# Two heads as two halves of the matmul array, and a reordered opening, in a hybrid decoder layer

## The reference

```python
mod = silu(c) @ w_ada + b_ada                       # shift1, scale1, gate1, shift2, scale2, gate2
h = rms_norm(x, g_norm1) * (1 + scale1) + shift1
z = h @ w_in                                        # qa ka va qb kb vb qi ki wi fl ga gb
# mixer A: index scores, top-k keys, attention with ALiBi; 8 heads of 64
s = einsum('bths,bth->bts', relu(einsum('bthd,bsd->bths', qi, ki) * 64**-0.5), wi)
oa = sparse_attend(qa, ka[sel], va[sel])            # sel = top_k(masked s)
# mixer B: forgetting attention; 8 heads of 64
ob = softmax(qb @ kb.T / 8 + Fq - Fk, causal) @ vb  # F = cumsum(log_sigmoid(fl + b))
merged = sigmoid(ga) * (oa @ w_o_a) + sigmoid(gb) * (ob @ w_o_b)
x = x + gate1 * (merged @ w_out)
h2 = rms_norm(x, g_norm2) * (1 + scale2) + shift2
y = x + gate2 * (square(relu(h2 @ w_up)) @ w_down)
```

## Time and profile before

| | us |
|---|---|
| median of 3 runs | 1118.53 |
| lowest and highest run | 1115.49, 1121.29 |
| the profiled execution | 1120.04 |
| its span, which all positions below count from | 1118.2 |
| PE busy | 1007.4 (90%) |
| DVE busy | 577.5 (52%) |
| ACT busy | 409.9 (37%) |
| POOL busy | 183.4 (16%) |
| first weight matmul starts | 44.61 |
| span of pair 2 (slot 0 to slot 0) | 36.8 |
| span of pair 7 | 35.9 |

### The profile page before, as it was taken

The page is one execution under the profiler, slowest core; times in us unless marked ns, Lnnn a source line. Parts: engine busy times, 40 slices in busy tenths (PEclk is TensorE's granted clock), DMA queues, the critical chain, the costliest instruction groups (busy, mean ns, idle before and its releaser), DMA issues.

```text
span 1118.2 us, 19588 instructions
## 1 busy us (share of the span) xinstructions
PE 1007.4 (90%) x7336; PEld 911.4 (82%) x7336; DVE 577.5 (52%) x1295; ACT 409.9 (37%) x818; POOL 183.4 (16%) x127
## 2 busy tenths in 40 slices
PE   5889988898989888649989999599989999998998
PEld 4687777787778778637489999589989999998998
DVE  2634899767575662563048844664433234442232
ACT  3355454444555442112065444344421124431111
POOL 4303223322342223320002322000000000000000
PEclk9799999999999999779979999799999999998999
DMA  9521521312222225774626665223323233332322
GB/s 323 165 79 32 163 76 48 87 45 62 56 67 57 59 57 160 246 233 135 207 85 198 193 201 173 76 57 95 94 76 94 83 87 93 94 94 75 88 64 77
DMA packets 186184, 124.51 MB, mean 111 GB/s; under 512 B 16499, under 2 KB 170163, under 8 KB 186116
## 3 DMA queue, kind: packets, MB, share of 16 engines
q1 hardware_dynamic: 185986, 123.50, 36.8%
q10 hardware_dynamic: 130, 0.10, 0.0%
HBM read 116.99 MB, written 6.59 MB: 111 GB/s over the span
## 4 chain that ended last, share of the span: by engine, by line
PE 74%; DVE 9%; DMA 5%; issue 4%; SPq 3%; ACT 3%; POOL 2%; ACTq 0%; DVEq 0%; POOLq 0%
PE bank L842 19%; PE bank L843 19%; PE bank L844 19%; PE bank L922 3%; PE bank L904 3%; DMA qbc<-q_d 3%; PE bank L1069 2%; PE bank L913 2%; POOL prod L772 1%; SPq L557 1%; DVE w_lo L1658 1%; PE bank L888 1%; PE bank L885 1%; PE bank L884 1%; PE bank L887 1%
## 5 line engine op out<-in xcount | busy, mean ns | idle before, releaser
L842 PE MATMUL bank<-h_hi,w_hi 128*128 128x260 f32 x1360 | 410.5, 302 | 29.0 <-issue 14.2
L843 PE MATMUL bank<-h_lo,w_hi 128*128 128x260 f32 x1360 | 394.8, 290 | 0.0
L844 PE MATMUL bank<-h_hi,w_lo 128*128 128x260 f32 x1360 | 393.9, 290 | 0.0
L842 PEld LDWEIGHTS bank<-h_hi,w_hi 128*128 128x128 f32 x1360 | 267.6, 197 | 37.9 <-issue 30.7
L843 PEld LDWEIGHTS bank<-h_lo,w_hi 128*128 128x128 f32 x1360 | 267.7, 197 | 4.1 <-issue 2.9
L844 PEld LDWEIGHTS bank<-h_hi,w_lo 128*128 128x128 f32 x1360 | 267.2, 196 | 0.0
L742 POOL TENSOR_TENSOR w_lo<-raw,w_hi 128x1024 fp32r<-128x1024 f32 x44 | 104.9, 2383 | 396.1 <-ACT w_hi L1259 229.6
L842 PE MATMUL bank<-u_hi,w_hi 128*128 128x260 f32 x512 | 147.0, 287 | 7.7 <-DVE u_lo L2046 7.7
L2031 DVE TENSOR_TENSOR w_lo<-raw,w_hi 128x1024 fp32r<-128x1024 f32 x62 | 76.0, 1226 | 146.2 <-ACT w_hi L1490 146.2
L843 PE MATMUL bank<-u_lo,w_hi 128*128 128x260 f32 x512 | 146.3, 286 | 0.0
L844 PE MATMUL bank<-u_hi,w_lo 128*128 128x260 f32 x512 | 146.3, 286 | 0.0
(11 more groups left out here) (319 smaller groups left out, 1384.0 us busy)
## 6 DMA issues: line engine op xcount, KB each, us to landing
raw<-in_w_in SPq DMA_DIRECT2D x44, 512.0 KB, 3.7
raw<-in_w_ada SPq DMA_DIRECT2D x32, 512.0 KB, 4.1
raw<-in_w_up SPq DMA_DIRECT2D x32, 512.0 KB, 3.8
raw<-in_w_down SPq DMA_DIRECT2D x32, 512.0 KB, 3.6
ada<-in_w_ada SPq DMA_DIRECT2D x4, 2048.0 KB, 13.6
kv<-in_cache_k_b SPq DMA_DIRECT2D x16, 256.0 KB, 3.1
qbc<-q_d SPq DMA_DIRECT2D x16, 256.0 KB, 4.1
kv<-in_cache_k_a SPq DMA_DIRECT2D x16, 256.0 KB, 3.4
```

The lines of the kernel that those rows point to most:

```text
L842: mm(out, hi[:, k, :], x_h, start=first and k == ks[0], stop=False)
L843: mm(out, hi[:, k, :], x_l, start=False, stop=False)
L844: end = mm(out, lo[:, k, :], x_h, start=False, stop=last and k == ks[-1])
```

## The change

Scores: `q_pad` gives way to `q_fm`, q of both heads without zeros. Each score product runs over 64 rows, the two heads' products one after the other into banks 4 and 5, both in the even slot of a pair of slots. A unit is now head U%2 and query block U%8//2, so the heads alternate. The products of index scores go in pairs in the same way. `values(U)` is now made for both heads and one query block at a time, in odd slots, in matmuls of 128 columns whose outputs are the two halves of bank 7. `store_back` and the stores of `q_idx` are one ACT instruction where they were two, and POOL zeroes neither buffer.

Opening: tile 0 is one DMA of 80 columns, and an ACT copy puts fl in its place; tile 2 is loaded ahead of the small constants. x is turned in two parts, chunks 0 to 3 ahead of the first c product and 4 to 7 between the second c product and the first weight tile. DVE scales all eight chunks, four and four. The first two weight tiles take chunks 0 to 3, then c products 2 and 3 with their turns follow on PE, then chunks 4 to 7.

```diff
@@ tile_dmas, dma_count
             if i == T_SMALL:
-                return [(dst[:, :, 0:HD], w_in_v[:, :, KI:KI + HD]), (dst[:, :, 64:64 + H], w_in_v[:, :, WI:WI + H]),
-                        (dst[:, :, ROW_FL:ROW_FL + H], w_in_v[:, :, FL:FL + H])]
+                return [(dst[:, :, 0:GA - KI], w_in_v[:, :, KI:GA])]
@@ gpsimd
-            pool.memset(q_idx[:, :, :], 0.0).then_inc(zeroed, 1)
...
-            for j in range(XN_DVE, NCH):
-                pool.tensor_tensor(xn[:, j, :], x_t[:, j, :], rs_all[:, :], ALU.mult).then_inc(xn_pool, 1)
...
-            pool.memset(q_pad[:, :, :, :], 0.0).then_inc(zeroed, 1)
@@ tensor, opening
+            turn_x(0)
+            turn_x(1)
             pe.wait_ge(c_landed, 16 * 5)
...
+            turn_x(2)
+            turn_x(3)
+            pe.wait_ge(cond_ready, 1)
+            mod_product(0)
             pe.wait_ge(diag_ready, 1)
...
+            pe.wait_ge(rs_all_ready, 1)
+            mod_turn(0)
+            mod_product(1)
+            turn_x(4)
+            turn_x(5)
+            mod_turn(1)
+            turn_x(6)
+            turn_x(7)
@@ first_tiles
                 for k in range(NCH):
+                    if k == 4 and not n:
+                        mod_product(2)
+                        mod_turn(2)
+                        mod_product(3)
+                        mod_turn(3)
@@ scores, values
             def scores(U):
-                p, hh, qb = U // 8, U // 4 % 2, U % 4
+                p, _, qb = unit(U)
                 if U >= 2:
-                    pe.wait_ge(lg_ready, U - 1)
+                    pe.wait_ge(lg_ready, U)
...
-                mm(bank[4 + U % 2][:, 0:width(qb)], q_pad[:, p % 2, hh, qb * P:(qb + 1) * P],
-                   k_fm[:, p % 2, 0:width(qb)], start=True, stop=True).then_inc(s_done, 1)
+                for hh in range(2):
+                    rows = slice(64 * hh, 64 * hh + 64)
+                    mm(bank[4 + hh][:, 0:width(qb)], q_fm[rows, p % 2, qb * P:(qb + 1) * P],
+                       k_fm[rows, p % 2, 0:width(qb)], start=True, stop=True).then_inc(s_done, 1)
...
-            def values(p, hh):
-                pe.wait_ge(pt_ready, 8 * p + 4 * hh + 4)
...
-                for kb in range(QB):
-                    last = mm(bank[7][64 * hh:64 * hh + 64, kb * P:SEQ], v_tok[:, p % 2, kb, 64 * hh:64 * hh + 64],
-                              p_t[:, hh, kb, kb * P:SEQ], start=kb == 0, stop=kb == QB - 1)
+            def values(U):
+                p, _, qb = unit(U)
+                pe.wait_ge(pt_ready, U + 2)
...
+                for kb in range(qb + 1):
+                    for hh in range(2):
+                        rows = slice(64 * hh, 64 * hh + 64)
+                        last = mm(bank[7][rows, qb * P:(qb + 1) * P], v_tok[:, p % 2, kb, rows],
+                                  p_t[:, qb % 2, hh, kb, :], start=kb == 0, stop=kb == qb)
@@ index_scores
                 if n >= 2:
-                    pe.wait_ge(idx_relu, n - 1)
+                    pe.wait_ge(idx_relu, n)
@@ pair loop on tensor
-                    for n in range(3 * s, 3 * s + 3):
+                    for n in range(3 * s + s % 2, 3 * s + 3, 2):
                         index_scores(n)
...
-                if 0 <= U < N_UNITS:
+                if 0 <= U < N_UNITS and U % 2 == 0:
...
-                if s == 6 and 1 <= p <= N_PAIRS:
-                    values(p - 1, 0)
-                if s == 2 and p >= 2:
-                    values(p - 2, 1)
+                if 0 <= U - 5 < N_UNITS and U % 2:
+                    values(U - 5)
@@ scalar
             mod_rows(0)
+            act.wait_ge(raw_landed[0], landed_value(0))
+            link(A(raw[:, 0, :, ROW_FL:ROW_FL + H], raw[:, 0, :, FL - KI:GA - KI], ACT.Copy))
+            round_w(0)
             mod_rows(1)
-            round_w(0)
+            store_x(4)
             round_w(1)
+            store_x(6)
...
-                if s == 2 and p >= 2:
+                if s == 3 and p >= 2:
                     round_o(p - 2)
@@ vector
             mod_add(0)
+            rest_w(0)
+            store_x(5)
             mod_add(1)
-            rest_w(0)
             rest_w(1)
-            dve.wait_ge(xn_dve, XN_DVE)
+            dve.wait_ge(xn_dve, 4)
             first_half(0)
+            store_x(7)
+            store_xs(1)
...
+            for j in range(4, NCH):
+                scale_x(j)
             mod_add(2)
             mod_add(3)
```

More of the change, by code:

```diff
@@ L203, in layer @@
         z = new("z", [P, 3, SEQ])
-        q_pad = new("q_pad", [P, 2, 2, SEQ])
+        q_fm = new("q_fm", [P, 2, SEQ])
+        place["at"] += 4096
         k_fm = new("k_fm", [P, 2, SEQ])
@@ L216, in layer @@
         pt_at = place["at"]
-        p_t = new("p_t", [P, 2, QB, SEQ])
+        p_t = new("p_t", [P, 2, 2, QB, P])
+        place["at"] += 8192
         ts_b, ts_at, ts_end = sb("ts_b", [NS, 4, SEQ])
@@ L528, in _ @@
             load_ada(3)
+            load(2)
             for half in range(2):
@@ L782, in _, with turn_x, mod_product, mod_turn @@
             pe.wait_ge(consts, 1)
+            pe.wait_ge(xs_landed, 16)
+            for g in range(2):
+                pe.wait_ge(x_landed[g], 16)
+            def turn_x(j):
+                if j == 7:
+                    pe.wait_ge(mod_row_ready, 1)
+                elif j >= 4:
+                    pe.wait_ge([xt_act, xt_dve][j % 2], (j - 4) // 2 + 1)
+                tr(bank[6][:, 8 * j:8 * j + 8], x_stok[:, j * P:(j + 1) * P], ident[0:NS, 0:NS])
+                for t in range(QB):
+                    last = tr(bank[X_BANK[j]][:, t * P:(t + 1) * P], x_tok[:, t, j * P:(j + 1) * P], ident[:, :])
+                last.then_inc(xt_done, 1)
+            def mod_product(t):
+                if t >= 2:
+                    pe.wait_ge(mod_row_ready, t - 1)
+                if t == 2:
+                    pe.wait_ge(xt_dve, 4)
+                pe.wait_ge(ada_landed[t], 16)
+                for r in range(2):
+                    for j in range(4):
+                        last = mm(bank[2 + t % 2][32 * j:32 * j + 32, :], cond_t[:, 4 * r + j, :], ada[:, t, 4 * r + j, :],
+                                  start=r == 0, stop=r == 1)
+                last.then_inc(mod_done, 1)
+            def mod_turn(u):
+                pe.wait_ge(mod_row_ready, u + 1)
+                if u:
+                    pe.wait_ge(mod_ready, u)
+                for q in range(4):
+                    last = mm(bank[7][:, 192 + 36 * u + 9 * q:192 + 36 * u + 9 * q + 9], mod_row[:, u % 2, q * P:(q + 1) * P], fold[:, :],
+                              start=True, stop=True)
+                last.then_inc(mod_turned, 1)
+            turn_x(0)
+            turn_x(1)
             pe.wait_ge(c_landed, 16 * 5)
@@ L956, in index_scores @@
                 if n >= 2:
-                    pe.wait_ge(idx_relu, n - 1)
-                mm(bank[4 + n % 2][:, 0:width(qb)], q_idx[:, h, qb * P:(qb + 1) * P], ki2[:, 0:width(qb)],
-                   start=True, stop=True).then_inc(idx_done, 1)
+                    pe.wait_ge(idx_relu, n)
+                for hh in range(2):
+                    rows = slice(64 * hh, 64 * hh + 64)
+                    mm(bank[4 + hh][:, 0:width(qb)], q_idx[rows, h // 2, qb * P:(qb + 1) * P], ki2[rows, 0:width(qb)],
+                       start=True, stop=True).then_inc(idx_done, 1)
             def side_step(e):
@@ L1231, in _ @@
             act.wait_ge(rs_spread, 1)
-            A(rs_all[:, SEQ:T], bank[1][:, 0:NS], ACT.Copy)
-            A(rs_all[:, 0:SEQ], bank[0][:, :], ACT.Copy).then_inc(rs_all_ready, 1)
+            A(rs_all[:, SEQ:T], bank[7][:, 136:136 + NS], ACT.Copy)
+            A(rs_all[:, 0:SEQ], bank[3][:, :], ACT.Copy).then_inc(rs_all_ready, 1)
             def mod_rows(t):
@@ L1296, in exps @@
             def exps(U):
[L1297 removed]
+                w = width(U % 8 // 2)
                 act.wait_ge(lg_ready, U + 1)
@@ L1376, in _ @@
                     c = i - T_QI
-                    if i == T_QI:
-                        act.wait_ge(zeroed, 2)
-                    A(q_idx[0:64, 2 * c, lo:hi], bank[half + 4 * par(i)][0:64, 0:hi - lo], ACT.Copy)
-                    last = A(q_idx[64:128, 2 * c + 1, lo:hi], bank[half + 4 * par(i)][64:128, 0:hi - lo], ACT.Copy)
+                    last = A(q_idx[:, c, lo:hi], bank[half + 4 * par(i)][:, 0:hi - lo], ACT.Copy)
                     if half == 1:
@@ L1581, in _ @@
             dve.wait_ge(rs_all_ready, 1)
-            dve.wait_ge(xt_act, 4)
-            dve.wait_ge(xt_dve, 5)
-            for j in range(XN_DVE):
-                dve.tensor_tensor(xn[:, j, :], x_t[:, j, :], rs_all[:, :], ALU.mult).then_inc(xn_dve, 1)
+            dve.wait_ge(xt_act, 2)
+            dve.wait_ge(xt_dve, 2)
+            dve.wait_ge(xs_dve, 1)
+            for j in range(4):
+                scale_x(j)
             def mod_add(t):
@@ L1883, in _ @@
                         normalize(p, s // 2 - 1)
-                if s == 3 and p >= 2:
+                if s == 4 and p >= 2:
```

148 lines of the change are left out of this document (61 added, 87 removed).

## The result

The changed kernel takes 1125.77 us (median of 11 runs, 1120.62 to 1130.97). The kernel before, in 11 runs beside it, takes 1119.16 us. The ratio is 1.0052, 95% interval 1.0028 to 1.0076: it is **slower by half a per cent**, where 1107 us had been forecast. The profiled execution took 1125.87 us with a span of 1123.9.

What follows compares the result with a forecast made beforehand. PE and its waits were taken to bound the kernel, DVE pairs 1 and 2. Terms -8.8, -1, +0.5 and -2 summed to -11.3 us, from 1118.53 to 1107 us; forecast band 1100 to 1113, range 1094 to 1121.

Steps and rivals of the forecast that it cites:

- Scores and values: Pair loop: halved products run side by side, scores -2.1 us and values -1.9 us a pair.
- rival 3: Scores and values: the halves don't run side by side, so the kernel is slower, 1139 us; chance 0.1.
- The switches: Pair loop: 8 excursions into the 64 column form instead of 2, +1.0 us a pair, bounds 0 and 1.6.
- The waits of slots 5 and 7: Pair loop: PE waits 2.4 and 2.7 us for ACT's store, 5.1 a pair against 3.0 before, +2.1 us a pair.
- pairs 3 to 8: Pair loop where PE and its waits bound: scores, values, switches and waits less cover, -8.8 us.
- The clock: Pair loop: three losses go, 4.8 us, and new waits bring 3 x 1.6, so the clock comes out even.
- Rival 2: Slots 5 and 7: low clock follows every new wait, +12.8 us, 1120; chance 0.18 together with half of rival 3.
- a clock below 0.93 in pairs 5 to 8: Pair loop: one of the signs named as showing the prediction wrong, a granted clock under 0.93 there.
- The index scores: Ahead of pair 1: halved products save 8 us but pairs wait for both banks, +0.5 us, bounds -0.5 and +3.
- The opening: Start to the end of tiles 0 and 1: they end at about 57 instead of 58.8, -2 us, bounds -5.5 and +3.
- Pairs 1 and 2: Pair loop where DVE bounds: its work is unchanged, slack 1 to 2 us each, -1 us for both.
- the pair loop: All pairs: -8.8 us for pairs 3 to 8 and -1 for the first two, -9.8 us.

Runs made afterwards that it cites:

- e5: Changed kernel with 8 matmuls whose result nobody reads ahead of the turned probabilities in slots 5 and 7; 1113.79 us, ratio 0.9941.
- e3: Changed kernel with 16 matmuls whose result nobody reads ahead of the turned probabilities in slots 5 and 7; 1127.85 us, ratio 1.0087.
- e9: Changed kernel with 8 unread matmuls in slots 5 and 7 and index scores one head at a time; 1107.27 us, ratio 0.9873.
- e6: Changed kernel with index scores one head at a time again, each on its half of the array; 1120.45 us, ratio 1.0013.
- e8: Changed kernel with p_t stored ahead of exps in even slots, rest_o first in slot 4, and single index scores; 1100.35 us, ratio 0.9825.
- e4: Kernel before with only the opening of the changed kernel; 1119.74 us, ratio 0.9990.
- e12: Kernel before with 8 matmuls whose result nobody reads in slot 5 of each pair; 1116.56 us, ratio 0.9967.
- e2: Kernel before with ACT's store of p_t ahead of exps in every slot; 1110.63 us, ratio 0.9923.
- e11: Changed kernel, single index scores; unread matmuls (slots 5, 7) in pairs 1 and 2, early p_t store and rest_o from pair 3; 1103.73 us, ratio 0.9861.

## Why the prediction was wrong, point by point

- **Scores and values: right in the products.** The scores of a pair take 0.42 + 0.63 + 0.85 + 1.06 = 3.0 us: 1.67 ns a column for both heads together and 0.21 us for each of the four excursions (the way into the 64 row form and back). One head alone took 0.86 / 512 = 1.68 ns a column, so the overlap is full, and rival 3, halves that don't overlap, is out. The values take 2.8 us (2.7 forecast): 0.37, 0.59, 0.81 and 1.02 us for 4, 8, 12 and 16 instructions, that is 0.15 us for the excursion and 0.054 for each instruction.
- **The switches: mis-sized.** Part of an excursion's price stands in the step ahead of it, which I had not looked at. One transpose of the probabilities takes 0.11 us ahead of the padded scores of the kernel before (352.01 to 352.12), and 0.20 us ahead of the new scores (360.70 to 360.90) and of the values (364.52 to 364.72):

```profile
352.01 0.27 PE L913 MATMUL bank<-ident,lg 128*128 128x128 f32 x1
```

```profile
360.70 0.27 PE L928 MATMUL bank<-ident,lg 128*128 128x128 f32 x1
360.90 0.70 PE L919 MATMUL bank<-k_fm,q_fm 64*128 64x256 f32 x4
...
364.52 0.27 PE L928 MATMUL bank<-ident,lg 128*128 128x128 f32 x1
364.72 1.09 PE L942 MATMUL bank<-p_t,v_tok 128*64 128x128 f32 x16
```

So an excursion costs 0.30 us for the scores and 0.24 for the values, and the eight of a pair 2.2 us. Less the two of before, which are some 0.25 us each, that is about +1.7, where +1.0 had been forecast with a bound of 1.6. PE's whole work in a pair can be read from e5's trace, which is at the full clock, with idle time and filling taken off. In pairs 5, 6 and 7 it is 2.3, 2.3 and 1.9 us shorter than before, where 3.0 had been forecast.

- **The waits of slots 5 and 7: right in place and sum.** 16 places with some 35 us in sum had been named, 15 with 34.9 came. In pair 7 they are 2.05 and 2.40 us, 4.5 a pair instead of 5.1; in slot 5 of pairs 1 and 2 they are 3.57 and 2.91, though no wait of 3.3 had been expected. By the windows of the earlier trace rows, pairs 3 to 8 held 19.6 us of waits before and not 17.9.
- **The clock: the step that failed.** "I price this as one loss in every second pair, 3 x 1.6, which makes the clock come out even." The trace has 15 slow half tiles with 20.7 us against 6 with 9.1: 11.6 us on the wrong side, and e3, e5 and e9, where the waits are filled, have none of them in the loop. I had put the point from which an idle time is followed by the low level at about 2.5 us, from one row of the opening and the harmless waits of 1.7. In the trace after, 2.05 us are enough in three of the four waits of that length, in slot 5 of pairs 5 to 8 (the half tiles behind 300.84 and 372.87 lost 1.6 each, that behind 336.15 lost 1.0, that behind 409.05 nothing), and even a wait of 1.86 us (345.66) has a half tile behind it that loses 1.0, where another of 1.86 (310.49) has none. The length does not decide it alone. In the trace after, 13 of the 15 waits have a slow half tile right behind them; in e6, with the same loop and 15 waits of 1.86 to 3.58 us, only nine; before, one of the six waits of 3.27 us and more has none (331.79), which the prediction doesn't mention; and in e8 one of 1.56 us (139.44) is followed by a loss of 1.6. What decides it is not shown. Rival 2 had this mechanism, with 12.8 us for it, and a chance of 0.18; it should have been the forecast. The condition I had named as one that would prove the prediction wrong, a clock below 0.93 in pairs 5 to 8, is met at 0.91 in pairs 6 and 7.
- **The index scores: wrong by size.** +0.5 had been forecast with bounds to +3, and 3.9 came, about one of it a slow half tile at its end. (The stretch before is also longer than I had put it: 24 times 0.77 is 18.4 us and not 17.) That DVE can't start before 125.6 held only as long as PE was there by then; in the trace after, PE's last index score ends at 125.9 behind a wait of 2.60 us. The waits of a pair for both banks were walked through at 1.1, 1.9 and 2.9 us, but the halved work was credited against them, although DVE and ACT, whose relus and sums are not halved, set the pace.
- **The opening: right in its steps, worth nothing in the time.** `first_half(0)` starts at 31.44 (29.7 forecast), tiles 0 and 1 end at 60.05 in this trace and at 55.6 in e8's (57 forecast). e4 can't be told from the kernel before.
- **Pairs 1 and 2:** 36.7 and 38.3 instead of 35.9 and 36.8, where -1 for both had been taken. Their waits of up to 3.57 us have slow half tiles behind them, which DVE's bound did not hide.

Where the forecast and the spans of the two traces part, stretch by stretch: the opening +2.3 instead of -2, the index scores +3.9 instead of +0.5, the pair loop +3.5 instead of -9.8, the rest -4.0 instead of 0. That is +5.7 instead of -11.3, and 13.3 of the 17.0 us between them lie in the loop. Within pairs 3 to 8 (-8.8 forecast, +1.2 measured), again with e5 as the measure of the work at the full clock, the work shrank by about 13.3 us and not 18.0, the waits grew by 5.8 (1.5 of it ahead of the last spread) and not 9.2, and the low clock took 8.7 more and not 0. So the two misses in work and waits nearly cancel, and the clock is what is left.

What the halves are worth without the clock can be seen in the pair loop of two pairs of traces: e9 against e12, both with filling, 293.7 against 301.4 us (e12 has two slow half tiles left in it, with 2.7 us, and e9 none), and e8 against e2, both with the early store, 288.2 against 295.5 (with about as much loss in slow half tiles, 4.5 and 4.8). That is -7.7 and -7.3 us where -9.8 had been forecast for the loop. Their ratios differ by some 10 and 11 us, but of the two differences in span 2.8 and 3.0 us lie in the opening, and in the second 4.4 behind the loop. What stays open is why the clock falls behind the wait in pair 3 of e11 and only 6 us later in e8; a single profile of each doesn't settle it.

## What to carry to other kernels

Count every wait that a change brings to PE twice: once by its length, and once by what the work behind it may cost at the low clock, even where the wait is only 2 us. Count a switch of the array's form in the step ahead of it too. Before two runs are compared, look at whether their traces have the same clock in the stretches that the edit does not touch. Saving PE's work in front of a wait that another engine ends saves nothing and may cost the clock; so mend the wait first. Look at what the releasing engine did while PE waited: here ACT stood idle in front of one instruction with the wanted one queued behind it, and an exchange of two lines made both kernels faster.
